# A router fed with raw residual rows, the last tile's normed rows made by ScalarE and GpSimd, and a fourth weight part on GpSimd

## What is computed

```
x   = x + gt1 * (concat([att, conv]) @ w_out)
h2  = rmsnorm(x, g_ffn) * (1 + sc2) + sh2            # modulate
aff = softmax(h2 @ w_router, axis=-1)                # 1024 x 16
g, idx = top_k(aff.T, 128)                           # each of 16 experts picks 128 tokens
xs  = h2[idx]
y   = (silu(xs @ w_gate[e]) * (xs @ w_up[e])) @ w_down[e] * g
x   = x + gt2 * segment_sum(y, idx)
out = rmsnorm(x, g_final)
```

## Time and profile before

| | |
|---|---|
| median of 3 runs | 2583.76 us (2581.22 to 2584.25) |
| the profiled execution | 2582.62 us |
| its span | 2581.0 us |
| mean granted TensorE clock | 0.979 |
| busy: PE, DVE, ACT, POOL | 2460.9, 1629.4, 1057.2, 214.1 us |

### The profile page before, as it was taken

The page is one execution under the profiler, slowest core; times in us unless marked ns, Lnnn a source line. Parts: engine busy times, 40 slices in busy tenths (PEclk is TensorE's granted clock), DMA queues, the critical chain, the costliest instruction groups (busy, mean ns, idle before and its releaser), DMA issues.

```text
span 2581.0 us, 30819 instructions
## 1 busy us (share of the span) xinstructions
PE 2460.9 (95%) x12081; PEld 2018.0 (78%) x12081; DVE 1629.4 (63%) x2028; ACT 1057.2 (41%) x1558; POOL 214.1 (8%) x224
## 2 busy tenths in 40 slices
PE   7999889999999999999999999989995999999996
PEld 6787568888888877888787898867684888888885
DVE  6999745225243645444443871477456999999987
ACT  4233434325131221121212522165244677777765
POOL 1000320000000000000000100000103011111100
PEclk9999889999999999999999999999996999999998
DMA  4111021220111322232222321110227899999988
GB/s 149 66 41 45 33 90 69 71 98 34 41 50 45 103 82 99 81 122 81 97 91 70 127 74 34 49 33 16 85 82 269 324 389 392 394 393 396 395 333 303
DMA packets 116413, 370.66 MB, mean 144 GB/s; under 512 B 6309, under 2 KB 15701, under 8 KB 116304
## 3 DMA queue, kind: packets, MB, share of 16 engines
q1 hardware_dynamic: 94832, 293.63, 29.9%
q0 software_dynamic: 21472, 75.51, 9.3%
HBM read 343.89 MB, written 25.26 MB: 143 GB/s over the span
## 4 chain that ended last, share of the span: by engine, by line
PE 84%; DVE 10%; ACT 3%; issue 2%; DMA 1%; POOL 1%; POOLq 0%; SPq 0%; ACTq 0%; DVEq 0%
PE banks L433 24%; PE banks L435 24%; PE banks L434 24%; DVE conv_out L1497 4%; DVE w_lo L427 2%; PE banks L2481 2%; PE banks L533 1%; PE banks L2529 1%; PE banks L2348 1%; PE banks L2327 1%; ACT w_hi L420 1%; PE banks L2498 1%; PE banks L2499 1%; PE banks L2606 1%; PE banks L2625 1%
## 5 line engine op out<-in xcount | busy, mean ns | idle before, releaser
L2015 DVE TENSOR_TENSOR expert_w_lo<-expert_w,expert_w_hi 128x2048 fp32r<-128x2048 f32 x189 | 426.9, 2286 | 29.9 <-ACT expert_w_hi L1337 28.4
L1337 ACT ACTIVATE expert_w_hi<-expert_w 128x2048 fp32r<-128x2048 f32 x192 | 366.7, 1918 | 151.9 <-PE banks L435 128.7
L433 PE MATMUL banks<-act_hi,w_hi 128*128 128x512 f32 x960 | 376.3, 392 | 7.3 <-DVE w_lo L427 4.1
L435 PE MATMUL banks<-act_hi,w_lo 128*128 128x512 f32 x960 | 374.1, 390 | 0.0
L434 PE MATMUL banks<-act_lo,w_hi 128*128 128x512 f32 x960 | 374.1, 390 | 0.0
L420 ACT ACTIVATE w_hi<-w_raw 128x1024 fp32r<-128x1024 f32 x152 | 156.9, 1060 | 299.1 <-PE banks L435 299.0
L427 DVE TENSOR_TENSOR w_lo<-w_raw,w_hi 128x1024 fp32r<-128x1024 f32 x152 | 181.6, 1222 | 140.5 <-ACT w_hi L420 136.1
L433 PE MATMUL banks<-w_hi,act_hi 128*128 128x512 f32 (+1 forms) x640 | 246.3, 385 | 6.6 <-DVE w_lo L427 3.0
L435 PE MATMUL banks<-w_hi,act_lo 128*128 128x512 f32 (+1 forms) x640 | 243.9, 381 | 0.0
L434 PE MATMUL banks<-w_lo,act_hi 128*128 128x512 f32 (+1 forms) x640 | 243.6, 381 | 0.0
L433 PEld LDWEIGHTS banks<-act_hi,w_hi 128*128 128x128 f32 x960 | 180.6, 188 | 47.7 <-issue 4.2
(11 more groups left out here) (404 smaller groups left out, 4164.0 us busy)
## 6 DMA issues: line engine op xcount, KB each, us to landing
expert_w<-in_w_gate SPq DMA_DIRECT2D x32, 2048.0 KB, 10.9
expert_w<-in_w_up SPq DMA_DIRECT2D x32, 2048.0 KB, 11.7
expert_w<-in_w_down SPq DMA_DIRECT2D x32, 2048.0 KB, 11.8
ada_w<-in_w_ada POOLq DMA_DIRECT2D x48, 512.0 KB, 4.0
w_raw<-in_mlp_up_w SPq DMA_DIRECT2D x16, 1024.0 KB, 5.4
w_raw<-in_mlp_down_w SPq DMA_DIRECT2D x16, 1024.0 KB, 5.0
w_raw<-in_w_in SPq DMA_DIRECT2D x10, 1024.0 KB, 5.3
w_raw<-in_w_in SPq DMA_DIRECT2D x18, 512.0 KB, 5.9
```

The source lines that it names most:

```text
L433: nc.tensor.matmul(o_, lh, rh, start=start, stop=False)
L435: return nc.tensor.matmul(o_, ll, rh, start=False, stop=stop)
L1337: act.activation(EWH[ring][:, 2 * j:2 * j + 2, :], EW[slot][:, 2 * j:2 * j + 2, :], ACT.Copy).then_inc(w_hi, 1)
L2015: dve.tensor_tensor(EWL[slot][:, c, :], EW[slot][:, c, :], EWH[ring][:, c, :], ALU.subtract).then_inc(w_ready, 1)
```

## The change

- **Router on raw rows.** The transposes take the residual tile `X` itself, in the middle (k = 4) of the next tile's product, and the router's product follows behind it, one tile earlier than before. The norm's gain goes into the router's weights (`WRG = WR * gain`), the shift into a row of constants (`RBI`, eight products of the shift, repeated over 128 columns, with `WR`), and VectorE scales the result by the row's inverse root and adds that row (`RLG`) before the maximum. Three strided loads bring gain, scale and shift by partition (`COLS`); `router_columns` on VectorE makes `WRG` and `SHB` ahead of tile 5 of the first half.
- **Last tile.** The normed rows of tile 7 are no longer made by VectorE's L518 and L522: ScalarE scales the row, GpSimd multiplies by the gain and adds the shift, then stores.
- **GpSimd makes four first lo parts**, two of them ahead of L938 to L944, two behind. VectorE's part 3 goes, and its expert rows' lo part comes first.
- **Merge.** The four small copies become a two-input maximum of a tile with itself; the copy in `chosen` becomes a multiplication by ones, and the cast of the token numbers goes into the addition.
- Filler products: 4, 2, 2, 2 instead of 6, 3, 3, 3.

```diff
-        def gemm_tokens(b, n0, lo=0, hi=NT, before=None, after=None, lhs=None, rhs_cols=(0, 512), lhs_k=None, ends=True):
+        def gemm_tokens(b, n0, lo=0, hi=NT, before=None, after=None, lhs=None, rhs_cols=(0, 512), lhs_k=None, ends=True, middle=None):
...
+                    if middle and k == 4:
+                        middle(t)
...
-        POOL_LO = 3
+        POOL_LO = 4
...
             pool.dma_start(WR[:, :, :], w_router_2[0].rearrange("(k p) n -> p k n", p=P)).then_inc(wr_in, 16)
+                for n, v in enumerate((g_ffn_2[0], mod_d[0, 4 * D:5 * D], mod_d[0, 3 * D:4 * D])):
+                    pool.dma_start(COLS[:, n, :], v.rearrange("(k p) -> p k", p=P)).then_inc(wr_in, 16)
...
             for t in range(NT):
                 pool.wait_ge(x3_new, t + 1)
                 pool.dma_start(acc_d[tok(t), :], X[:, t, :]).then_inc(x3_out, 16)
-                pool.wait_ge(nm_xn, N_EXP + t + 1)
-                pool.dma_start(h2_d[tok(t), :], XN[:, t % 2, :]).then_inc(h2_out[t % 2], 16)
+                if t < NT - 1:
+                    h2_store(t)
+            xl = XN[:, 1, :]
+            pool.wait_ge(l7_xs, 1)
+            pool.tensor_tensor(xl, xl, GAIN[:, :], ALU.mult).then_inc(l7_xs, 1)
+            pool.wait_ge(l7_xs, 2)
+            pool.tensor_tensor(xl, xl, SHIFT[:, :], ALU.add).then_inc(nm_xn, 1)
+            h2_store(NT - 1)
...
+            first_lo(0)
+            first_lo(1)
             row(GT2[:, :], mod_d[0, 5 * D:6 * D], gt2_in)
...
-            for n in range(POOL_LO):
-                slot, c = n // 2, slice(2 * (n % 2), 2 * (n % 2) + 2)
-                pool.wait_ge(w_hi, W_SPLIT + n + 1)
-                pool.tensor_tensor(EWL[slot][:, c, :], EW[slot][:, c, :], EWH[slot][:, c, :], ALU.subtract).then_inc(w_ready, 1)
+            first_lo(2)
+            first_lo(3)
...
+            i7 = N_EXP + NT - 1
+            act.wait_ge(nm_tp, 2 * (i7 - 1))
+            act.activation(XN[:, 1, :], X[:, NT - 1, :], ACT.Square, accum_out=SS[:, i7:i7 + 1]).then_inc(nm_sq, 1)
+            h2_copy(NT - 1)
+            router_exp(NT - 2)
+            act.wait_ge(nm_sq, i7 + 1)
+            act.activation(SD[:, i7:i7 + 1], SS[:, i7:i7 + 1], ACT.Sqrt, bias=EPSC[:, 0:1], scale=1.0 / D).then_inc(nm_sd, 1)
+            router_exp(NT - 1)
+            act.wait_ge(l7_rs, 1)
+            act.activation(XN[:, 1, :], X[:, NT - 1, :], ACT.Copy, scale=RS[:, i7:i7 + 1]).then_inc(l7_xs, 1)
...
             def router_max(t):
                 dve.wait_ge(rt_r, t + 1)
-                dlink(dve.tensor_reduce(RST[:, 2, t:t + 1], BK[6 + t % 2][:, 0:NE], AX, ALU.max))
+                dlink(dve.scalar_tensor_tensor(out=RLG[:, t % 2, :], in0=BK[6 + t % 2][:, 0:NE], scalar=RS[:, N_EXP + t:N_EXP + t + 1],
+                                               in1=RBI[:, :], op0=ALU.mult, op1=ALU.add))
+                dlink(dve.tensor_reduce(RST[:, 2, t:t + 1], RLG[:, t % 2, :], AX, ALU.max))
...
-            dve.tensor_copy(MRG[0:32, :], SRT[64:96, ::-1])
-            dlink(dve.tensor_copy(MRG[32:64, :], SRT[96:128, ::-1]))
+            dve.tensor_tensor(MRG[0:32, :], SRT[64:96, ::-1], SRT[64:96, ::-1], ALU.max)
+            dlink(dve.tensor_tensor(MRG[32:64, :], SRT[96:128, ::-1], SRT[96:128, ::-1], ALU.max))
...
-                dlink(dve.tensor_copy(GGS[:, lo:hi, :], BK[bank][:, 5 * lo:5 * hi].rearrange("p (e n) -> p e n", n=5)))
-                dlink(dve.tensor_tensor(TIDF[:, lo:hi], GGS[:, lo:hi, 0], GGS[:, lo:hi, 1], ALU.add))
-                dve.tensor_copy(GI[:, lo:hi], TIDF[:, lo:hi]).then_inc(tk_out, 1)
+                dlink(dve.tensor_tensor(GGS[:, lo:hi, :].rearrange("p e n -> p (e n)"), BK[bank][:, 5 * lo:5 * hi],
+                                        ONEB[:, 0:n5], ALU.mult))
+                dve.tensor_tensor(GI[:, lo:hi], GGS[:, lo:hi, 0], GGS[:, lo:hi, 1], ALU.add).then_inc(tk_out, 1)
...
             dve.wait_ge(w_ready, W_SPLIT + POOL_LO)
-            w_piece_lo(3, 1, 1, 1)
             expert_rows_lo(0)
...
+            for k in range(8):
+                m = pe.matmul(BK[7][:, 256:256 + NE], SHB[:, k, :], WR[:, k, :], start=(k == 0), stop=(k == 7))
+            m.then_inc(sel_c, 1)
+            gemm_tokens(B_W2 + 1, T_W2 + 8, middle=lambda t: rows_x3_T(t - 1) if t >= 1 else None,
+                        after=lambda t: router(t - 1) if t >= 1 else None)
+            rows_x3_T(NT - 1)
+            router(NT - 1)
...
-                turn_over(6 if e == 0 else 3)
+                turn_over(4 if e == 0 else 2)
```

More of the change, by code:

```diff
@@ L683, in build @@
         ex_u = sem("ex_last_up")
+        l7_rs, l7_xs = sem("last_tile_root"), sem("last_tile_scaled")
         LASTE = NE - 1
@@ L927, in _, with h2_store @@
             pool.dma_start(WR[:, :, :], w_router_2[0].rearrange("(k p) n -> p k n", p=P)).then_inc(wr_in, 16)
+            with nc.allow_non_contiguous_dma(reason="1024 gains, scales and shifts by partition"):
+                for n, v in enumerate((g_ffn_2[0], mod_d[0, 4 * D:5 * D], mod_d[0, 3 * D:4 * D])):
+                    pool.dma_start(COLS[:, n, :], v.rearrange("(k p) -> p k", p=P)).then_inc(wr_in, 16)
+            def h2_store(t):
+                pool.wait_ge(nm_xn, N_EXP + t + 1)
+                pool.dma_start(h2_d[tok(t), :], XN[:, t % 2, :]).then_inc(h2_out[t % 2], 16)
             for t in range(NT):
@@ L1929, in router_norm, with root, rows, router_columns @@
                 dve.tensor_scalar(AFFALL[:, t, 0:NE], REX[:, t % 2, :], RST[:, 3, t:t + 1], None, ALU.mult).then_inc(rt_a, 1)
+            def root(i):
+                dve.wait_ge(nm_sd, i + 1)
+                dlink(dve.reciprocal(RS[:, i:i + 1], SD[:, i:i + 1]))
+            def rows(i, src):
+                xn = XN[:, i % 2, :]
+                dlink(dve.scalar_tensor_tensor(out=xn, in0=src, scalar=RS[:, i:i + 1], in1=GAIN[:, :], op0=ALU.mult, op1=ALU.mult))
+                dve.tensor_tensor(xn, xn, SHIFT[:, :], ALU.add).then_inc(nm_xn, 1)
+            def router_columns():
+                dve.wait_ge(wr_in, 64)
+                dlink(dve.scalar_tensor_tensor(out=COLS[:, 1, :], in0=COLS[:, 1, :], scalar=1.0, in1=COLS[:, 0, :],
+                                               op0=ALU.add, op1=ALU.mult))
+                dve.tensor_tensor(WRG[:, :, :], WR[:, :, :], COLS[:, 1, :].unsqueeze(2).to_broadcast([P, 8, NE]), ALU.mult)
+                dve.tensor_copy(SHB[:, :, :], COLS[:, 2, :].unsqueeze(2).to_broadcast([P, 8, P])).then_inc(sel_c, 1)
             for half in range(2):
@@ L1934, in _ @@
                     dve.wait_ge(sel_c, 4)
+                    dve.tensor_copy(RBI[:, :], BK[7][:, 256:256 + NE])
                     dve.tensor_scalar(IOTA[:, :], BK[7][:, 0:P], 1.0, None, ALU.add)
                     dve.tensor_copy(RSEL[:, :, :, 1], BK[7][:, P:P + 1].unsqueeze(2).to_broadcast([P, NT, NE]))
[L1937 to L1950, removed]
-                        else:
[L1952 to L1958, removed]
@@ new lines, in _ @@
+                for t in range(NT):
+                    if t == 5 and half == 0:
+                        router_columns()
+                    if t == 7 and half == 0:
+                        split_lo(B_W2 + 1)
+                    n = T_W2 + 8 * half + t
+                    dve.wait_ge(x2_in[t], 32)
+                    dve.wait_ge(acc_ready, n + 1)
+                    xs = X[:, t, 512 * half:512 * (half + 1)]
+                    tmp = T1[:, n % 2, :]
+                    dve.tensor_tensor(tmp, acc(n), GT1[:, 512 * half:512 * (half + 1)], ALU.mult).then_inc(acc_dve, 1)
+                    dve.wait_ge(acc_dve, freed(n)[1])
+                    i_ = dve.tensor_tensor(xs, xs, tmp, ALU.add)
+                    if half == 1:
+                        i_.then_inc(x3_new, 1)
+                    else:
+                        dlink(i_)
+                    if half == 1 and t >= 1:
+                        root(N_EXP + t - 1)
+                        if t < NT - 1:
+                            rows(N_EXP + t - 1, X[:, t - 1, :])
+                            router_max(t - 1)
+                        else:
+                            router_max(t - 1)
+                            rows(N_EXP + t - 1, X[:, t - 1, :])
+                        router_norm(t - 1)
@@ L1960, in _ @@
+            dve.wait_ge(nm_sd, N_EXP + NT)
+            dve.reciprocal(RS[:, N_EXP + NT - 1:N_EXP + NT], SD[:, N_EXP + NT - 1:N_EXP + NT]).then_inc(l7_rs, 1)
+            dve.wait_ge(l7_rs, 1)
+            router_max(NT - 1)
+            router_norm(NT - 1)
             dve.wait_ge(rt_at, 1)
@@ L2541, in router, with rows_x3_T @@
                 if t >= 2:
-                    pe.wait_ge(rt_e, t - 1)
-                else:
-                    pe.wait_ge(wr_in, 16)
+                    pe.wait_ge(rt_m, t - 1)
                 for k in range(8):
-                    m = pe.matmul(BK[6 + t % 2][:, 0:NE], HTR[:, t % 2, k, :], WR[:, k, :], start=(k == 0), stop=(k == 7))
```

(13 more changed lines are left out.)

42 lines of the change are left out of this document (26 added, 16 removed).

## The result

The changed kernel takes 2592.09 us in the median (2590.96 to 2593.26) against 2582.53 us for the kernel before, eight runs of each. The ratio that the comparison gives is 1.0031 (95%: 1.0022 to 1.0041), +8.0 us (+9.6 by the two medians): slower, and near the forecast of 2591. The profiled execution took 2591.22 us for a span of 2589.5, clock 0.977.

A forecast was written before the change was run, and what follows sets the result against it. TensorE bounds the kernel; changes between w_out's last product and expert 0 reach the end one for one. Merge end +8.0 (including the router's -2.6), select row -0.19: +7.8 on 2582.6 gives 2590.4, or 2591.5 against the median; said 2591, range 2580 to 2594.

The forecast's parts named there:

- First half: TensorE in w_out's second half: earlier transposes, router and row-constant products and restarts, less one wait, end the last product +3.3 us.
- The tail: Tile 7 from its last w_out product to the last exponential: 1960.5 against 1963.10, a gain of 2.6 us (2.4 to 3.3).
- GpSimd's queue: GpSimd's steps after the last exponential: lo parts 2 and 3 fall right on VectorE's merge, which starts 16.8 us after it.
- X: Start of ScalarE's last exponential in the router, forecast at 1960.5 us; GpSimd's queue and the merge are counted from it.
- The price of the meeting: VectorE's merge and GpSimd alternate by whole instructions; merge ends at X+32.0 against X+21.7 without waits, +8.0 us against before.
- The copies: The merge's four small copies made two-input steps: 0.28 us each for 0.22, 0.3 in all; the skill's rule says it buys nothing.
- Edits at nothing: Fewer fillers and VectorE's lost lo part 3 gain nothing; a clock not up would delay expert 0 by up to 2.4 us.
- rival D: A or C with TensorE's late clock ahead of expert 0 as well: +5 to +10.5 us, chance 0.08.
- A: The forecast itself: two GpSimd lo parts stand in VectorE's merge, +7.8 us (6 to 9.5), chance 0.53.
- The distance to the end: From expert 0's first product to the end of the execution: unchanged at 581 us.
- B: Not slower: the merge's small steps slip past GpSimd as the sorting rounds do, -2.5 us, chance 0.24.
- C: One part only: VectorE, once in, keeps GpSimd out through the merge; one wait of 4.5 us, +3 in all, chance 0.15.

The follow-up runs named there:

- a_lo2: The changed kernel with GpSimd making lo parts 0 and 1 only and VectorE making parts 2 and 3: 2582.65 us, ratio 1.0002 to the kernel before.
- b_lo4: The kernel before with GpSimd making four lo parts instead of three, VectorE's part 3 gone, router untouched: 2588.70 us, ratio 1.0026.
- b_lo4_two: The kernel before with four lo parts on GpSimd and the merge's four small copies as two-input maxima: 2588.23 us, ratio 1.0021.
- a_fill: The changed kernel with the old 6, 3, 3, 3 filler products: 2589.16 us, ratio 1.0032 to the kernel before.
- v_two: The changed kernel with two lo parts on GpSimd ahead of its small steps, plain merge copies and 6, 3, 3, 3 fillers: 2583.57 us, ratio 0.9995.
- a_split: The changed kernel with GpSimd's lo parts 2 and 3 cut into four instructions of 512 columns each: 2592.12 us, ratio 1.0029 to the kernel before.
- v_one: The changed kernel with one lo part on GpSimd, VectorE making parts 1 to 3, plain merge copies and 6, 3, 3, 3 fillers: 2581.55 us, ratio 0.9989.
- v_hold: v_one plus five products of constants on TensorE ahead of expert 0's hidden transposes: 2580.55 us, ratio 0.9985 to the kernel before.

## Why the prediction was right, point by point

- **First half, +3.3: measured +2.8.** The wait before the first transposes went as said. The row-constant product cost 1.78 from its start to that of the next product (1887.88 to 1889.66) for the forecast 1.69. The restarts were over-sized: with the transposes in the middle a tile takes (1947.12 - 1906.15)/5 = 8.19 against the 8.16 of the earlier trace rows, so seven tiles cost 0.2 and not 0.8. The 0.34 of a first step was taken for 0.11 lost at each extra break; the tiles show 0.03.
- **The tail, gain 2.6: measured 3.3**, the upper bound. 0.5 of the 0.7 more is the first half's, and the rest the router product, 3.27 where I had half clock throughout (3.61). It began 3.7 us behind the end of w_out's last product (1950.53 + 0.39), forecast 3.8. By the Trainium skill (ScalarE: Activation LUTs, What ACT_TABLE_LOAD costs) each load has a drain of 1.38 us more. The trace after does not show it either: the root starts 0.02 us after the load of 1.28 ends.
- **GpSimd's queue from X.** Lo parts 2 and 3 were forecast at X+18.5 to X+27.5 alone. They ran from X+18.9 to X+27.9, in the merge. The merge's start was forecast at X+16.8 and was X+16.9. This is the step that the result hangs on, and it held within 0.4 us.
- **The price of the meeting.** Forecast: merge end X+32.0, measured X+30.8. Turn-taking by whole instructions is right, two parts met two steps, and a_lo2 gives 8.5 us for them. Over-sized were the small steps' turns: about 1.2 forecast, some 0.5 by a_lo2. I had also let GpSimd's parts wait for VectorE; they lose next to nothing (8.96 for two beside the merge, 9.00 for two beside the rounds). So the parts ended at X+27.9 for the played-out X+28.6, and what was left behind them took 2.9 for 3.4, since four pairs were left and not six and a half.
- **The copies.** The exchange buys nothing: b_lo4 and b_lo4_two have waits of 4.35 and 4.43 us. No row of before could show it. By the Trainium skill (SBUF — State Buffer, Who interferes with whom) a copy in its two-port mode contends with GpSimd; whether this reversed copy of 32 x 128 ran in it, no run here shows.
- **Edits at nothing: the fillers were not nothing.** The sum went with full clock ahead of expert 0 and left a late clock, up to 2.4 us, to rival D (0.08). It came: +2.0 between the transposes and expert 0's first product. a_fill gives 1.9 of it back. So A was right for the merge, but it was A with D's addition, and the +7.8 was met (+7.9) because this error and the two over-sized terms cancel: 0.7 more gain, 1.2 less merge, 2.0 more clock. The mechanism was right; that the number was met so closely is luck.
- **The distance to the end, 581.** Measured 582.6. The clock fell in expert 1 behind a wait that before has too (2.31 us, and the clock stayed up). In the profiles it fell in after, a_lo2, a_fill, b_lo4_two, v_two and a_split, and not in before, b_lo4, v_one and v_hold. b_lo4 and b_lo4_two differ in four small VectorE steps only, so it is no plain property of the change. By the next transposes of expert rows, after is 1.2 us behind before (49.99 for 48.74 from expert 0's first product); the other 0.5 lie later. How often each kernel falls into it stays open.
- **The rivals.** B (no wait) and C (one wait) are excluded for this change by its two long steps. But the row on which C rested stays: at 258.52 GpSimd's step waited through a run of VectorE steps of two inputs, 1.27 us each, that ended at 262.68, and ended at 263.26 itself; it got no turn in between. So one to one is how this merge and its variants behave, and not every meeting. What decides it no run here shows. B's assumption, that small steps slip past GpSimd as the rounds do, holds for the rounds only: sixteen rounds again took 15.2 us (1960.34 to 1975.58) under two parts. In b_lo4 there is one wait of 4.35, but only because one part meets the merge; it is no case of C.

## What to carry to other kernels

Before giving GpSimd more work, lay its queue beside VectorE's on a common clock, and count, for each GpSimd instruction that overlaps a chain of small VectorE steps like these (copies, maxima and minima; not the sorting rounds), its whole length on that chain. Cutting it into pieces or changing the steps' form did not get it back here; moving it off the chain did. A chain that gets shorter moves its successors too: here the router's gain brought the merge forward onto parts that a later queue had pushed back. And products that only keep TensorE busy have a price when removed, which is read from the clock of the stretch behind them and not from their own time.

## What the hardware showed that I had not expected

- A plain reversed copy of 32 x 128 with one input waits for a GpSimd step as a two-input step does (4.35 us for 0.22), while MAX8 and MATCH_REPLACE8, of one input from SBUF, run at 0.98 us a round under the same GpSimd parts, and at 0.98 without them (v_one, behind 1976.46).
- The turns in the merge are strictly one to one: eight GpSimd instructions of 512 columns held eight VectorE steps of 0.2 us for 1.19 to 1.31 each. GpSimd itself took 9.82 us for eight quarters against 8.96 for two wholes; how much of that is waiting is not shown, since a step of 512 columns took 1.27 elsewhere, and eight of that are more than 9.82.
- TensorE's clock behind waits of 1.7 to 3.0 us is not decided by the length of the wait: behind the same 1.68 it fell to 0.50 in a_lo2 and a_fill and stayed at 1.00 in b_lo4, and it fell behind 2.10 (after) and stayed behind 1.93 (v_one) and 2.31 (before). With products of constants in the gap it stayed up in the one execution profiled (v_hold).
